# Three unused tensors in the memory plan of a two-block float32 kernel on one core

## What is computed

```python
mod = silu(c) @ w_ada + b_ada                      # 6 x 1024, and 2 x 1024 more at the end of block 1
h = modulate(rms_norm(x, norm1_w), sh1, sc1)
p = h @ w_in                                       # q, k, v, z, decays, short-conv and gate columns
o = gated_delta_rule_chunked(q, k, v, g, beta)     # 8 heads, chunks of 64
y_a = (rms_norm(o) * silu(z)) @ w_gdn_proj
y_b = (gb * conv(gc * xin)) @ w_sc_out
x = x + g1 * ((gate_a * y_a + gate_b * y_b) @ w_o)
h = modulate(rms_norm(x, norm2_w), sh2, sc2)
x = x + g2 * ((silu(h @ w_g) * (h @ w_u)) @ w_ffn_out)
x = modulate(rms_norm(x, normf_w), shf, scf)
qkv = rms_norm(x) @ w_qkv                          # block 2: 16 heads, one block of 256 keys
x = x + attention(q, k, v, rel_bias) @ w_o2
u = conv(rms_norm(x) @ w_up)
x = x + (silu(u_gate) * u_val) @ w_down
out = rms_norm(x)
```

## The kernel before

| tensors | first byte | past a multiple of 128 |
|---|---|---|
| `wh0` to `wl4`, every 4,096 bytes | 41,088 | 0 |
| `HH`, `HL` | 90,240, 98,432 | 0 |
| `cst` | 108,384 | 96 |
| `acc`, `tmp`, `sq` | 113,184 and on | 32 |
| `QT`, `KT`, `V` and the rest of `mixer` up to `YH`, `YL` | 131,616 and on | 32 |
| `FH`, `FL`, `FH2`, `FL2` | 152,608, 175,136, 131,616, 154,144 | 32 |
| `QA`, `KA`, `VA`, `OHh`, `OLl` | 154,688 and on | 64 |

## Time and profile before

### The profile page before, as it was taken

One profiled execution on the slowest core, in us unless ns is written; L12 is line 12 of the kernel. 1 busy time (PEld: TensorE's weight loads), 2 busy tenths in 40 slices (PEclk: granted clock), 3 DMA queues, 4 the chain that ended last, 5 costly groups with the idle time before them and its releaser, 6 DMA issues.

```text
span 951.3 us, 18526 instructions
## 1 busy us (share of the span) xinstructions
PE 910.9 (96%) x7968; PEld 867.1 (91%) x7968; DVE 673.4 (71%) x1131; ACT 500.2 (53%) x809; POOL 63.9 (7%) x86
## 2 busy tenths in 40 slices
PE   5689998999999999999999999999999999999997
PEld 2588888898999999999999999999888999999997
DVE  3878676567679988678797775587656678777643
ACT  2477566645344465555354444466556476665442
POOL 0101111101200000020000000120000100000002
PEclk9799999999999999999999999999999999999999
DMA  8743321232249986455987779525322445545631
GB/s 334 267 172 120 127 95 45 93 131 90 90 140 331 356 302 245 173 192 182 290 317 269 274 277 247 211 92 219 133 100 97 160 156 200 177 178 172 238 123 45
DMA packets 27681, 177.31 MB, mean 186 GB/s; under 512 B 2864, under 2 KB 5680, under 8 KB 7504
## 3 DMA queue, kind: packets, MB, share of 16 engines
q1 hardware_dynamic: 27600, 176.13, 52.4%
HBM read 174.29 MB, written 1.84 MB: 185 GB/s over the span
## 4 chain that ended last, share of the span: by engine, by line
PE 85%; DVE 7%; ACT 6%; DMA 1%; issue 1%; SPq 0%; DVEq 0%; ACTq 0%
PE ps L1073 47%; PE ps L1079 23%; PE ps L1071 2%; PE ps L1118 1%; PE ps L1126 1%; DVE wl L1818 1%; ACT wh L1431 1%; PE ps L1212 1%; PE ps L1129 1%; PE ps L1229 1%; PE ps L1280 1%; PE ps L1077 1%; DVE KT L1700 1%; DMA raw<-in_ada_dram 1%; DVE tmp L1957 1%
## 5 line engine op out<-in xcount | busy, mean ns | idle before, releaser
L1073 PE MATMUL ps<-HH,wh 128*128 128x256 f32 x1480 | 385.0, 293 | 2.6 <-DVE wl L1818 2.1
L1818 DVE TENSOR_TENSOR wl<-raw,wh 128x1024 fp32r<-128x1024 f32 x265 | 322.1, 1236 | 82.8 <-ACT wh L1431 82.6
L1073 PE MATMUL ps<-HH,wl 128*128 128x256 f32 x1480 | 372.4, 284 | 0.0
L1431 ACT ACTIVATE wh<-raw 128x1024 fp32r<-128x1024 f32 x265 | 272.9, 1041 | 170.4 <-PE ps L1079 112.8
L1073 PEld LDWEIGHTS ps<-HH,wh 128*128 128x128 f32 x1480 | 284.9, 192 | 11.4 <-issue 3.6
L1073 PEld LDWEIGHTS ps<-HH,wl 128*128 128x128 f32 x1480 | 285.2, 193 | 1.9 <-issue 1.9
L1079 PE MATMUL ps<-HL,wh 128*128 128x256 f32 x1480 | 235.3, 284 | 0.0
L1079 PEld LDWEIGHTS ps<-HL,wh 128*128 128x128 f32 x1480 | 203.9, 193 | 0.0
L1073 PE MATMUL ps<-FH,wl 128*128 128x256 f32 x352 | 86.9, 280 | 0.0
L1073 PE MATMUL ps<-FH,wh 128*128 128x256 f32 x352 | 86.9, 280 | 0.0
L1717 DVE SCALAR_TENSOR_TENSOR acc<-raw,silc,acc 128x512 f32<-128x512 f32 x101 | 76.7, 759 | 8.5 <-DMA raw<-in_ada_dram 5.4
(11 more groups left out here) (264 smaller groups left out, 1060.4 us busy)
## 6 DMA issues: line engine op xcount, KB each, us to landing
raw<-in_ada_dram SPq DMA_DIRECT2D x32, 1024.0 KB, 5.2
raw<-in_w_fi_dram SPq DMA_DIRECT2D x22, 1024.0 KB, 4.9
raw<-in_w_up_dram SPq DMA_DIRECT2D x22, 1024.0 KB, 4.8
raw<-in_w_rest_dram SPq DMA_DIRECT2D x20, 1024.0 KB, 4.8
raw<-in_w_in_dram SPq DMA_DIRECT2D x16, 1024.0 KB, 4.9
raw<-in_w_qkv_dram SPq DMA_DIRECT2D x12, 1024.0 KB, 4.9
raw<-in_w_o_dram SPq DMA_DIRECT2D x8, 1024.0 KB, 4.8
raw<-in_w_fo_dram SPq DMA_DIRECT2D x8, 1024.0 KB, 4.9
```

Source lines behind the costliest of these rows:

```text
L1073: e.matmul(o, w[:, k, 128 * t:128 * t + 128], x_hi[:, k0 + k, :], start=first and n + k == 0, **MM)
L1431: e.activation(whl[u % HALF][0][:, 0:n], raw[i % RAW][:, c:c + n], ACT.Copy).then_inc(*a_hi.up(u))
L1818: e.tensor_tensor(wl[:, 0:n], raw[i % RAW][:, c:c + n], wh[:, 0:n].bitcast(F32), ALU.subtract).then_inc(*v_lo.up(u))
```

## The change

Three tensors that nothing reads or writes are added to the memory plan, of 64, 96 and 96 bytes per partition. No instruction, wait or transfer is added, removed or reordered; addresses move.

```diff
     whl = [(sb(f"wh{i}", [128, 1024], F32R), sb(f"wl{i}", [128, 1024], F32R)) for i in range(HALF)]
     X = sb("X", [128, 8, T])
+
+    sb("home_x", [128, 16])
     HH = sb("HH", [128, 8, T], F32R)
     HL = sb("HL", [128, 8, T], F32R)
...
     sqs = [sb(f"sq{i}", [128, 512]) for i in range(3)]
 
+    sb("home_y", [128, 24])
     mixer = ExitStack()
     QT = sb("QT", [128, 8, T], where=mixer)
...
     r3c = sb("r3c", [128, 2], where=phase)
+    sb("home_o", [128, 24], where=phase)
     QA = sb("QA", [128, 8, T], where=phase)
```

## The result

| | before | after |
|---|---|---|
| median of six runs | 953.23 us (952.06 to 956.14) | 945.41 us (943.94 to 946.77) |
| ratio, with its 95% interval | | 0.9915 (0.9897 to 0.9932) |
| profiled execution, and its span | 953.1, 951.3 us | 946.8, 945.0 us |

The change gains 7.8 us, 0.8%. The sign was forecast, the size was not: 30 us were forecast, and the time lies above the range (915 to 937). Further down, ratios and gains of a kernel are against runs of the kernel before on the same chip. A time called "one run" was measured once, and its total carries less than the paces read from its trace.

A forecast was written before the change was run, and what follows sets the result against it. TensorE's matmul stream was taken to bound the kernel. Gross 37.4 us less 1.6, 0.8, 3.0 and 2.0 left 30.0: 953.1 to 923.1 in the profiled execution, 924 us as the median, range 915 to 937.

The forecast's parts named there:

- The sign: Whole kernel: faster was given 0.90, same 0.07, slower 0.03.
- What bounds the kernel: Whole kernel: TensorE's matmuls cover 96% of the span, so time taken from its stream is taken from the kernel.
- The distance counts, and not the row's own remainder: Products, priced in v2: the distance between streamed row and weights sets the pace; 1.3 us there, otherwise nothing.
- the price of `HH`: HH and HL products, 4,440 matmuls: from 120.0 to OHh's 113.3 ns, 6.7 ns each, 29.7 us.
- `HH` at any other pace than `OHh`: Changed profile: this outcome would show the forecast wrong; spacings of 113 to 114 ns were expected in ug/uv.
- The other terms: Remaining products: FH to FL2 gain 4.3 us, YH and YL 2.1, v2 1.3, OHh and OLl 0.
- The costs taken at nothing: VectorE, ScalarE and a few transposes: taken as 0; bounds 2 us either way and 0.8 us either way.
- What the stream doesn't pay out: Deductions from the gross 37.4 us: 1.6, 0.8, 3.0 and 2.0 us, leaving 30.0.
- the wait on VectorE's part of the weights: gb, z and scout, line 1818 between 330 and 370 us: TensorE's lead runs out, 2.0 us lost.
- the chains of the delta rule and attention: Between 60 and 280 us: chains through VectorE and ScalarE don't shorten, 3 us lost, between 0 and 10.
- Half of it: Rival for HH and v2: pattern period longer than 128, pace 117.4 ns, gain 12 us, 942 us; chance 0.05.
- Nothing happens: Rival for the whole kernel: OHh is fast for another reason, time stays at 954 us; chance 0.06.

The follow-up runs named there:

- The 14 splits: Kernel after the change with 14 matmuls, at chosen product starts, each cut into two of 128 columns: 936.44 us, ratio 0.9818 to the kernel before.
- The kernel at 112: Against the kernel before, the HH, YH, FH and FH2 pairs at distance 112 from the weights, OHh still at 64: 931.23 us, ratio 0.9754.
- e3_d128: Against the kernel before, everything from HH on moved by 128 bytes, so no remainder by 128 changes: 951.39 us in one run.
- h2_fine: Against the kernel before, distances in fine steps: HH at 120, YH 104, FH 124, FH2 108, OHh 64: 960.15 us in one run.
- all at 112: HH, YH, FH and FH2 pairs at distance 112, and OHh and OLl there too, against the kernel before: 930.97 us, ratio 0.9765.

## Why the prediction was wrong in size

**What bounds the kernel: right.** TensorE's stream does. After the change 8.7 us of spacings became 6.3 us of span and 7.8 us of the median; in the profiled execution 0.6 us went to a later first product (39.5 us into the span, 38.9 before). The 14 splits gained about 9.0 us net in the spacings and 10.5 us of the median.

**The distance counts, and not the row's own remainder: right.** Moving the weights did to `HH` what moving `HH` did. The Trainium skill says in "TensorE: Matmul & The Clock Gate" (what happens when you issue a matmul) that the streamed operand and the weights have a read port each. By that the distance would be worth nothing. The runs disagree with this reading: one instruction stream had paces from 113.3 to 121.1 ns in `ug`/`uv` after changes of addresses alone. That the ports are what collides isn't shown by it.

**The failed step** is the price of `HH`: "I price them at the pace of `OHh`, which is the same pair of remainders: 120.0 - 113.3 = 6.7 ns each, 29.7 us." It took a pace to be a property of the pair of places. At distance 64 there are two paces, 113.3 and 117.8 ns. Which one holds can change where the stream breaks off, where it passes to another tensor, and at a split of one matmul. `HH` came out at 117.8: 2.2 ns x 4,440 = 9.8 us in place of 29.7. The 113.3 of the earlier trace rows was `OHh`'s in one execution; in a second one of the same kernel its last 155 spacings had 117.8. The prediction's own sign for this step, "`HH` at any other pace than `OHh`", would not have caught it: in the kernel after `OHh` has 117.3 on average, nearly `HH`'s pace.

**The other terms.** `FH` and `YH` hung on the same price. Forecast were 4.3 and 2.1 us, measured -0.5 and 0.2, because 32 had already given 117.3 and 118.1 to 118.7 ns on average. `v2` was put at 1.3 us and gave 0.9: some of its stretches took the faster pace. `OHh` was put at 0 and cost 0.7. Their sum is 9.8 - 0.5 + 0.2 + 0.9 - 0.7 = 9.7 us, of which 8.7 were found in the spacings (some 250 of `HH`'s lie outside them, as the forecast left out 240).

**The costs taken at nothing** held: VectorE and ScalarE are busy for 672.7 and 500.4 us, 673.4 and 500.2 before.

**What the stream doesn't pay out** can't be judged from the change, which made it only 9 us shorter. The kernel at 112 is the test. Of 28.4 us 21.0 reached the span, so 7.4 were lost; the forecast had taken off the same 7.4 of its 37.4. The place foreseen for the wait on VectorE's part of the weights was right too: the longer new wait for `wl` lies in `ga`, and the two are worth 1.8 us where 2.0 were taken. Of the rest, the growth of the three longer waits shown is 1.4 us, and 0.7 us is a later first product (39.6 us into the span, 38.9 before). The last 3.5 us were not found; the forecast had put 3.0 on the chains of the delta rule and attention. That the two sums of 7.4 agree is in part luck, since the forecast's parts were not all found.

**The rivals.** "Half of it" named 942, 3 us from the result, with a price near the right one: `HH` at 117.4 ns. Its mechanism, that 64 above the weights is another place than 64 below, isn't what the runs show: `OHh`, at its old place, has 117.8 too. Its premise, that the remainder by 128 doesn't say all, was right (`e3_d128`). "Nothing happens" for the reason that `OHh` was fast by something else than its place was half right in the same manner. The two had 0.11 together, too little for evidence in which one stage of 192 matmuls stood for 4,440.

**The sign** was right, at 0.8% and past the 0.5% that a measurement can tell.

**What stays open.** Why a stream takes one of two paces, and what a distance acts on; no view of the trace shows it. Why `v2` is slow at distance 112. Why the stage of the delta rule stays at 116.9 ns with `HH` at 112. How the addresses count beyond the remainder by 128.

## What to carry to other kernels

When matmuls and weight loads alternate without a pause, read the pace from starts, stage by stage, and try the distance between the streamed rows and the weights in steps of 16 bytes: in this kernel that alone was worth 2.4%, and no multiple of 32 was as good as 112. Take it as a search and not as a rule: one stream at 112 stayed slow. Before a pace that one short stage shows is put on the whole kernel, look for it in a second execution, and see whether it changes within a stage at equal addresses. A forecast with such a price needs the other pace of the same place as a rival with a large chance.

## What the runs showed of the chip that was not expected

- Two lasting paces at one pair of addresses (distance 64): steps of 113, 113, 114 ns, or of 117 to 119 with a mean of 117.8. The pace changed at breaks of TensorE's product stream, at a passage from one tensor to another without a break, and at one matmul cut in two (0.105 us); none of these changed it each time.
- The mean pace by distance, for 256 columns and 128 x 128 weights at the full clock: 120 ns at 0, 80, 104 and 108; 119.3 at 8 (`v2` of `h2_fine`); 118.3 or 120.0 at 96; 116.7 to 118.7 at 32, 48 and 124; 113.3 or 117.8 at 64; 113.3 to 119.9 at 16; 121.1 at 120; 113.3 at 112 in calm stages, but 116.9 in the delta rule's stage and 118.7 in `v2`. Each holds for the tensors that stood there and their addresses; 128 bytes more changed 120.0 to 118.7, and 117.3 to 116.7.
- The duration of one matmul in these timelines is 0.28 us at 113.3 ns as at 120. Means in ns do move a little with the pace (`HL`: 284 in the kernel before, 281 in the kernel after; 277 in the last group of `HH` and `HL` with all at 112), but the pace itself has to be read from the starts.
